# Token-major blocks multiplied as pairs of 512 columns, and an embedding product from high and low parts

## The reference, cut to what matters

```python
# first block, end
x = x + jnp.einsum('bse,ed->bsd', mixed, w_out[layer])      # mixed is [1024, 2048]
return rms_norm(x, final_norm_w)
# second block
h = x @ w_in[i]                                              # h[..., B_V_OFFSET:...] are the attention's values
...
merged = jax.nn.sigmoid(ga) * (ya @ w_branch_a[i]) + jax.nn.sigmoid(gb) * (yb @ w_branch_b[i])
mix_out = merged @ w_out[i]
ple = jax.nn.sigmoid(x @ w_ple_gate[i]) * (p[i] @ w_ple[i])  # p[i] is [1024, 256], w_ple is [256, 1024]
x = layer_norm(DEEPNORM_ALPHA * x + mix_out + ple, ln_g[i], ln_b[i])
```

## Time and profile before

| | us |
|---|---|
| median of 3 runs | 2396.09 (2396.05 to 2398.22) |
| profiled execution, its own time | 2396.95 |
| its span | 2395.2 |
| PE busy | 2337.4 (98%) |
| DVE busy | 1314.2 (55%) |
| ACT busy | 911.5 (38%) |
| POOL busy | 780.2 (33%) |

### The profile page before, as it was taken

One profiled execution on the slowest core, in us unless ns is written; L12 is line 12 of the kernel. 1 busy time (PEld: TensorE's weight loads), 2 busy tenths in 40 slices (PEclk: granted clock), 3 DMA queues, 4 the chain that ended last, 5 costly groups with the idle time before them and its releaser, 6 DMA issues.

```text
span 2395.2 us, 39157 instructions
## 1 busy us (share of the span) xinstructions
PE 2337.4 (98%) x15544; PEld 2049.8 (86%) x15544; DVE 1314.2 (55%) x2648; ACT 911.5 (38%) x1678; POOL 780.2 (33%) x705
## 2 busy tenths in 40 slices
PE   8999999999999999999999999999999999999998
PEld 7889978798888899999888899888899888887798
DVE  4003269999997433271232655456455455577536
ACT  5124654444444432232222333333333334455320
POOL 3121334445654221222443343243243242232112
PEclk9999999999999999999999999999999999999999
DMA  6234334343334422132333524314324314475621
GB/s 245 96 121 163 139 130 151 124 142 115 115 128 165 175 97 80 53 124 102 110 106 117 184 72 150 115 71 150 115 71 150 115 71 181 142 266 185 222 86 71
DMA packets 139053, 312.23 MB, mean 130 GB/s; under 512 B 12288, under 2 KB 55936, under 8 KB 127616
## 3 DMA queue, kind: packets, MB, share of 16 engines
q1 hardware_dynamic: 80192, 223.85, 27.5%
q10 hardware_dynamic: 58688, 86.00, 9.9%
HBM read 211.77 MB, written 98.04 MB: 129 GB/s over the span
## 4 chain that ended last, share of the span: by engine, by line
PE 88%; DVE 8%; issue 1%; ACT 1%; DMA 1%; POOL 0%; DVEq 0%; ACTq 0%; SPq 0%
PE bank L410 12%; PE bank L412 12%; PE bank L411 12%; PE bank L421 9%; PE bank L422 8%; PE bank L423 8%; PE bank L2486 3%; PE bank L2509 3%; PE bank L1853 3%; PE bank L1851 3%; PE bank L1852 3%; PE bank L1470 1%; PE bank L2475 1%; PE bank L734 1%; PE bank L2791 1%
## 5 line engine op out<-in xcount | busy, mean ns | idle before, releaser
L410 PE MATMUL bank<-at_hi,w_hi 128*128 128x512 f32 x1408 | 581.7, 413 | 2.3 <-DVE stage L2017 0.9
L412 PE MATMUL bank<-at_hi,w_lo 128*128 128x512 f32 x1408 | 552.3, 392 | 0.0
L411 PE MATMUL bank<-at_lo,w_hi 128*128 128x512 f32 x1408 | 550.9, 391 | 0.0
L421 PE MATMUL bank<-w_hi,at_hi 128*128 128x256 f32 x1792 | 520.7, 291 | 0.8 <-issue 0.8
L376 POOL TENSOR_TENSOR w_lo<-w_raw,w_hi 128x2048 fp32r<-128x2048 f32 x69 | 318.4, 4614 | 594.6 <-ACT w_hi L389 570.5
L423 PE MATMUL bank<-w_hi,at_lo 128*128 128x256 f32 x1792 | 508.4, 284 | 0.0
L422 PE MATMUL bank<-w_lo,at_hi 128*128 128x256 f32 x1792 | 508.4, 284 | 0.0
L421 PEld LDWEIGHTS bank<-w_hi,at_hi 128*128 128x128 f32 x1792 | 345.3, 193 | 7.4 <-issue 5.6
L422 PEld LDWEIGHTS bank<-w_lo,at_hi 128*128 128x128 f32 x1792 | 344.9, 192 | 0.8 <-issue 0.2
L423 PEld LDWEIGHTS bank<-w_hi,at_lo 128*128 128x128 f32 x1792 | 344.5, 192 | 0.0
L410 PEld LDWEIGHTS bank<-at_hi,w_hi 128*128 128x128 f32 x1408 | 268.4, 191 | 64.1 <-issue 11.7
(11 more groups left out here) (313 smaller groups left out, 3849.8 us busy)
## 6 DMA issues: line engine op xcount, KB each, us to landing
w_raw<-in_weights SPq DMA_DIRECT2D x84, 1024.0 KB, 7.4
feat<-stage ACTq DMA_DIRECT2D x184, 256.0 KB, 2.0
tok<-stage ACTq DMA_DIRECT2D x72, 256.0 KB, 2.2
stage<-feat SPq DMA_DIRECT2D x32, 256.0 KB, 3.6
w_mem<-in_w_mem SPq DMA_DIRECT2D x4, 1024.0 KB, 5.8
x<-in_x SPq DMA_DIRECT2D x4, 1024.0 KB, 11.8
logg<-gate_g ACTq DMA_DIRECT2D x8, 512.0 KB, 3.0
rec_b<-logg SPq DMA_DIRECT2D x16, 256.0 KB, 5.6
```

What stands on the lines that cost most here:

```text
L410: nc.tensor.matmul(ps_gemm[i % 2], wh, ah, start=(k == 0), stop=False)
L411: nc.tensor.matmul(ps_gemm[i % 2], wh, al, start=False, stop=False)
L412: last = nc.tensor.matmul(ps_gemm[i % 2], wl, ah, start=False, stop=(k == KT - 1))
L421: nc.tensor.matmul(o, ah, wh, start=(k == 0), stop=False)
```

## The change

Token-major weights are taken as a pair: `w_hi2` and `w_lo2` are [128, 2, 8, 256], and one matmul moves both blocks' 256 columns, 512 in all (`pair_tile`). `pair_pass` goes through the 8 k-tiles outside and four token tiles inside, in four banks (`LEFT` is `ps_fill`, `RIGHT` is `ps_gemm`, `ps_6` and `ps_7`). High and low parts of a pair are made by halves of k (`pair_high`, `pair_low`), the first half once the pass before has gone through its first four k-tiles. The very first half pass stays at 256 columns (`entry_pass`). The 16 groups of four transposes stand inside the passes (`TURNS_B`, `TURNS_V`). The first quarter block's weights are split by halves too.

The embedding's product becomes six float32r matmuls from parts. In the first round PE makes it ahead of tile n, in the second behind it. Its operands are loaded and the first parts made in the mixing stage; the later ones (`ple_input_high`, `ple_input_low`) stand in ACT's and DVE's order of `p9`.

```diff
+        def pair_high(act, g, part):
+            if part == 0:
+                act.wait_ge(half_used, HALVES_BEFORE + pair_number(g) - 1)
+            else:
+                act.wait_ge(tile_done, 4 * g + 8)
+            for b in range(2):
+                act.wait_ge(w_loaded[b], (g // 2 + 1) * 16)
+            k = chunk(part)
+            nc.scalar.activation(w_hi2[:, :, k, :], w_raw[:, :, k, :], ACT.Copy).then_inc(w_high, 1)
...
+        def pair_tile(bank, h, k, n):
+            o = bank.rearrange("p (b n) -> p b n", b=2)
+            tok = slice((CH * h + n) * P, (CH * h + n + 1) * P)
+            ah, al, wh, wl = at_hi[:, k, tok], at_lo[:, k, tok], w_hi2[:, :, k, :], w_lo2[:, :, k, :]
+            nc.tensor.matmul(o, ah, wh, start=(k == 0), stop=False)
+            nc.tensor.matmul(o, ah, wl, start=False, stop=False)
+            return nc.tensor.matmul(o, al, wh, start=False, stop=(k == KT - 1))
...
         def p4_pe(pe):
+            entry_pass(pe, OUT_A, LEFT, lambda n: None, FILLED1)
+            pe.wait_ge(c_mx, 4 * PAIRS + 4)
+            pe.wait_ge(tile_out, 4 * OUT_A + 2)
+            pair_pass(pe, OUT_A, 1, RIGHT, lambda n: None, FILLED1)
+            pair_pass(pe, OUT_B, 0, LEFT, lambda n: pe.wait_ge(tile_out, 4 * OUT_A + n + 3))
+            pair_pass(pe, OUT_B, 1, RIGHT, lambda n: pe.wait_ge(tile_out, 4 * OUT_A + n + 7),
+                      beside=lambda k, n: turn_after(pe, TURNS_B, k, n))
+            pair_pass(pe, VALUES_A, 0, RIGHT, lambda n: pe.wait_ge(tile_out, 4 * OUT_B + n + 7), FILLED2,
+                      beside=lambda k, n: turn_after(pe, TURNS_V, k, n))
...
         def p5_act(act):
             s = gemm2[0]
+            for n in range(CH):
+                pair_evacuate(act, s, 0, n, RIGHT)
+            differences_high(act, range(1))
+            pair_high(act, VALUES_B, 0)
+            differences_high(act, range(1, 3))
+            pair_high(act, VALUES_B, 1)
+            for n in range(CH):
+                pair_evacuate(act, s, 0, CH + n, LEFT)
+            differences_high(act, range(3, 4))
+            for n in range(CH):
+                pair_evacuate(act, s, 1, n, RIGHT)
+            act.wait_ge(fill_lo, FILLED3)
+            sums_high(act, 0)
+            for part in range(2):
+                first_loaded_high(act, part)
+            for n in range(CH):
+                pair_evacuate(act, s, 1, CH + n, LEFT)
             for m in range(Q_N):
                 quarter_results(act, m)
...
+        def embedding_product(pe, it, n):
+            pe.wait_ge(e_out, it * 8 + (n + 1))
+            pe.wait_ge(ple_low, PLE_LOWS + 9 * it + n + 2)
+            for k in range(2):
+                ph, pl, wh, wl = pT_hi[:, n % 2, k, :], pT_lo[:, n % 2, k, :], wple_hi[:, k, :], wple_lo[:, k, half(it)]
+                nc.tensor.matmul(ps_fill[n % 2], ph, wh, start=(k == 0), stop=False)
+                nc.tensor.matmul(ps_fill[n % 2], ph, wl, start=False, stop=False)
+                last = nc.tensor.matmul(ps_fill[n % 2], pl, wh, start=False, stop=(k == 1))
+            last.then_inc(e_prod, 1)
...
-            with pe.Fori(0, 2) as it:
+            for it in range(2):
                 for n in range(8):
+                    if not it:
+                        embedding_product(pe, it, n)
                     for part in range(PARTS):
                         gemm_part(pe, s, it, n // 4, n % 4, part,
                                   (lambda k, h: FILLED3 + (2 + h) * KT + k) if n < 4 else None)
+                    if it:
+                        embedding_product(pe, it, n)
...
@@ merge @@
             nc.vector.tensor_tensor(to, a, b, ALU.add).then_inc(m_out, 1)
+            if n < 7:
+                ple_input_low(dve, it, n + 1)
             dve.wait_ge(e_gate, it * 8 + (n + 1))
...
             nc.vector.scalar_tensor_tensor(x, x, ALPHA, e, ALU.mult, ALU.add).then_inc(e_out, 1)
+            if (it, n) == (0, 7):
+                ple_weights_low(dve, 1)
+                ple_input_low(dve, 1, 0)
```

More of the change, by code:

```diff
@@ L189, in build @@
                 mpb = sb("merge_b", [P, 2, HALF], F32, part)
+                pT_hi, pT_lo = [sb(f"ple_{n}", [P, 2, 2, P], F32R, part) for n in ("hi", "lo")]
         mga, mgb, pT = stage[:, 0:2], stage[:, 2:4], fill
@@ new lines, in pair_pass @@
+        def pair_pass(pe, g, h, banks, free, filled=None, beside=None):
+            for k in range(KT):
+                if h == 0 and k % (KT // 2) == 0:
+                    pe.wait_ge(w_split, g + k // (KT // 2) + 3)
+                if filled is not None:
+                    pe.wait_ge(fill_lo, filled + h * KT + k + 1)
+                for n in range(CH):
+                    if k == 0:
+                        free(n)
+                    last = pair_tile(banks[n], h, k, n)
+                    if k == KT - 1:
+                        last.then_inc(tile_done, 1)
+                    elif h and (k, n) == (KT // 2 - 1, CH - 1):
+                        last.then_inc(half_used, 1)
+                    if beside:
+                        beside(k, n)
@@ L1806, in p4_pe @@
-        def p4_pe(pe):
[L1807 to L1813, removed]
-        def p4_pool(pool):
[L1816 to L1821, removed]
+            residual_norm(dve, 7)
@@ L2056, in p5_pe @@
         def p5_pe(pe):
[L2057 to L2065, removed]
+            pair_pass(pe, VALUES_A, 1, LEFT, lambda n: pe.wait_ge(fill_lo, FILLED2 + KT + CH + n + 1), FILLED2)
+            pair_pass(pe, VALUES_B, 0, RIGHT, lambda n: pe.wait_ge(tile_out, 4 * VALUES_A + n + 3))
+            pair_pass(pe, VALUES_B, 1, LEFT, lambda n: pe.wait_ge(tile_out, 4 * VALUES_A + n + 7))
             for m in range(Q_N):
@@ L2218, in p5_pool @@
         def p5_pool(pool):
-            for g in range(gemm2[0].first + 2, Q_AT):
-                split_low(pool, g // 2, g % 2)
-            for m in range(Q_N):
+            for part in range(2):
+                pair_low(pool, VALUES_B, part)
+            first_weight_lows(pool)
+            for m in range(1, Q_N):
                 weight_lows(pool, m)
@@ L2650, in mixing_dve @@
             branch_mixed(dve, it, 1)
+            if last:
+                ple_weights_low(dve, 0)
+                ple_input_low(dve, 0, 0)
             branch_gate(dve, it, 1)
```

236 lines of the change are left out of this document (175 added, 61 removed).

## The result

The changed kernel takes 2413.38 us (median of 6 runs, 2410.9 to 2417.84) against 2396.85 for the kernel before: a ratio of 1.0067, 95% interval 1.0056 to 1.0077, or about +16 us. The forecast was slower, 2404.3, in a range of 2394 to 2413; the direction is right, the size is half of what came (+8.2 for +16.5), and the median lies 0.4 us above the range's upper end.

What follows compares the result with a forecast made beforehand. PE was taken as the bound, busy 2337.4 of 2395.2 us. The terms -7.7 - 8.4 + 2.2 - 5.6 + 12.6 + 7.6 + 3.5 + 4.0 sum to +8.2 us, giving 2404.3 us, in a range of 2394 to 2413.

Steps and rivals of the forecast that it cites:

- Matmul distance: Token-major stage: 1344 matmuls of 256 columns become 672 of 512, 0.2286 us apart instead of 0.240 per pair: -7.7 us.
- rival (3): Token-major blocks: two runs of 256 columns cost as much as two matmuls; 2412.0 us, chance 0.10.
- Transposes in the passes: Rest of the token-major stage: sixteen transpose groups between matmuls, 8.1 to 8.2 us in place of 16.6: -8.4 us.
- The wait ahead of the ninth group: Token-major stage: PE reaches the ninth transposes before DVE's last scaling ends, an estimated 0.7 us (0 to 4.6).
- Start of the quarter products: After the last value pass: PE's third product waits for ACT, which first empties four banks: +2.2 us, lower bound 0.
- Embedding's product: Last stage: six matmuls take 1.37 us in place of 1.72, sixteen times: -5.6 us.
- The new wait: Last stage: PE waits for DVE's low parts at products 2 to 7, product 1 and the second round's start: +12.6, +7.6, +3.5.
- the six alike: Last stage, first round: PE waits 2.1 us for DVE's low part at each of products 2 to 7, +12.6 us.
- the turn's wait: Turn to the last stage's second round: PE waits for low parts behind merge 7's last operation, +3.5 us.
- Clock: Last stage: product 1's wait and the turn's wait each bring a fall of PE's clock: +4.0 us (0 to 5.2).
- rival (4): Last stage: the six 2.1 us waits bring three more clock falls of 1.7 to 2.4 us; 2410.4 us, chance 0.12.
- Theory O: Experiments' rival theory: the additional clock falls have another source in the changed kernel than PE's waits for low parts; no chance given.

Runs made afterwards that it cites:

- the last experiment: The token-major half of the change alone, with each matmul of 512 columns issued as two of 256: 2392.65 us, ratio 0.9977 to the kernel before.

## Why the prediction was right in direction and short in size

- *Matmul distance, -7.7.* Right. 7.6 by the last experiment. Two runs of 256 columns cost 0.227, like one of 512 and a little less than the 0.2286 taken; rival (3) is out. The Trainium skill ("TensorE: Matmul & The Clock Gate", Part 1) gives 215.7 ns for back-to-back matmuls of 512; the passes here stayed at 227.
- *Transposes in the passes, -8.4.* Right, 9.0 by the same experiment. The wait ahead of the ninth group was forecast as 0.7 and is 0.53.
- *Start of the quarter products, +2.2.* Right: 1.8. In six of the eight traces with this wait a fall of the clock came behind it (1113.6 to 1117.0 in that of the changed kernel), about 1.7 us, which the forecast did not reckon with.
- *Embedding's product, -5.6.* Right: six starts of 0.227 are 1.36 in place of 1.72, 5.8 in all.
- *The new wait, 12.6 + 7.6 + 3.5.* Right: 12.0, 7.39 and 3.36, 22.8 for 23.7 (24.0 counted as distances, as the forecast did), and DVE's low part takes 0.42. Three experiments show the cause: the six alike go when the product is moved behind the tile, or (five of them) the low part ahead of DVE's wait, and come with the embedding half alone. That the turn's wait hangs on POOL, too, is read from the rows; no experiment took POOL's subtraction away: in the changed kernel DVE's L3082 starts at 2256.46, behind POOL's subtraction at 2256.34, and lasts 5.02. POOL's row first, then DVE's:

```profile
2256.34 4.59 POOL L381 TENSOR_TENSOR w_lo<-w_raw,w_hi 128x2048 fp32r<-128x2048 f32 x1 [36.57 <-ACT w_hi L394]
```

```profile
2256.46 5.02 DVE L3082 SCALAR_TENSOR_TENSOR X<-X,ple_gate 128x512 f32<-128x512 f32 x1
2261.41 1.21 DVE L2995 TENSOR_TENSOR wple_lo<-wple,wple_hi 128x1024 fp32r<-128x1024 f32 x1
2262.54 0.41 DVE L3009 TENSOR_TENSOR ple_lo<-fill,ple_hi 128x256 fp32r<-128x256 f32 x1
```

- *Clock, +4.0.* This is the term that was mis-sized, and it holds most of the miss of 8.3 us. The prediction said that the waits of 2.1 us "are just under what brought none", from one wait of 2.26 without a fall, and counted two falls. Four of the six waits of 2.0 brought one, too: 23 us at the lower clock, where the falls it went by had 6.9 and 3.4, and 10.4 us lost in that stage instead of 4.0. It is what rival (4) described, with a chance of 0.12, three falls and a price of 2410.4; with the 1.7 behind the quarter wait it comes to 2412.1, near the measured 2413.4. The other terms together came out about 1 us cheaper than forecast. The step failed because one wait without a fall was taken for a limit: a wait of 2.2 to 2.3 us for DVE's `da_k_lo`, which stands in all eleven traces, has a fall behind it in six of them, the changed kernel's among them, and none in five, that of the kernel before among them. Theory O was wrong: with the waits gone, the clock in the last stage is 1.00.

Open is what makes PE's wait for `rec_mx` 1.7 us or more in some executions and 1.5 or less in others, in a stage that the change doesn't touch. In the traces the token-major stage begins between 913.0 and 920.9 us, which is of the size of the spread between the runs of one kernel (3 to 13 us). Nothing was tried on it. Open is also why the same wait, in the same place, brings a fall in one execution and none in another.

## What to carry to other kernels

If an operation is moved ahead of a tile so that PE has something to do, look at who makes its operands, and what that engine waits for in its queue: here the operand stood behind the result of the tile that PE had just finished, and 22.8 us of waits followed. A wait on PE has two prices, its own length and the matmuls at half clock behind it; here eight waits of 24.0 us in all cost 10.4 more by the second. A change made of two halves should be timed as two: one of these was worth -14 us, the other +29. With the product behind its tile and its parts made early, the second half gains, too, and with ACT's banks emptied later both give the best kernel, at 0.9902 of the time before.

## What was not expected of the hardware

A wait of PE of 1.7 to 2.0 us can be enough for the granted clock to fall to 1.2 GHz, and need not be. The waits from 1.7 to 2.3 us in the eleven traces, by what PE waited for:

| wait of PE | us | fall behind it | none |
|---|---|---|---|
| the six alike for low parts, changed kernel and embedding half alone | 2.0 | 8 | 4 |
| low parts, product behind the tile | 2.02, 2.06 | 1 | 1 |
| partial copy, quarter products | 1.7 to 1.8 | 6 | 2 |
| `rec_mx` | 1.70 to 1.87 | 12 | 4 |
| DVE's `da_k_lo` | 2.2 to 2.3 | 6 | 5 |
| transposes, kernel before and embedding half alone | 2.26 | 0 | 2 |

No wait of 1.53 us or less for `rec_mx` or a low part had one. The length of the wait alone doesn't sort these rows.

A DVE update of `X` with two SBUF operands that began behind a POOL subtraction was held in every case seen (4.66, 5.02 and 4.71 in the changed kernel, at 2215.65, 2256.46 and 2287.86, and 5.05 above, for 0.69). The Trainium skill's "SBUF — State Buffer" (Who interferes with whom) says that a DVE instruction with two SBUF inputs contends with a GpSimd instruction that reads SBUF; the trace agrees. What is new is only that a reordering that has nothing to do with POOL can put such a stall ahead of something that PE waits for.
